# Spreading an expert's rows over the slots of its half in a top-2 mixture-of-experts block on one core

## The reference

```python
def hierarchical_moe(v, grp_w, grp_b, exp_w, exp_b, w_gate, w_up, w_down):
    ...
    grp_p, grp_idx = lax.top_k(grp_prob, 1)                  # 1 of 4 groups
    ...
    top_w, top_idx = lax.top_k(exp_prob, TOP_K_IN_GROUP)     # 2 of its 8 experts
    ...
        hg = jax.nn.silu(jnp.einsum('td,edf->tef', t, w_gate[g])) * jnp.einsum('td,edf->tef', t, w_up[g])
        hg = hg * combine[:, g, :, None].astype(hg.dtype)
        out = out + jnp.einsum('tef,efd->td', hg, w_down[g]).astype(F32)
```

## Time and profile before

| | us |
|---|---|
| median of 3 runs | 512.49 (511.51 to 515.82) |
| the profiled execution, its span | 512.3 |
| PE busy | 477.8 |
| DVE busy | 232.3 |
| ACT busy | 169.8 |
| POOL busy | 149.9 |

### The profile page before, as it was taken

The page is one execution under the profiler, slowest core; times in us unless marked ns, Lnnn a source line. Parts: engine busy times, 40 slices in busy tenths (PEclk is TensorE's granted clock), DMA queues, the critical chain, the costliest instruction groups (busy, mean ns, idle before and its releaser), DMA issues.

```text
span 512.3 us, 7264 instructions
## 1 busy us (share of the span) xinstructions
PE 477.8 (93%) x2718; PEld 264.5 (52%) x2718; DVE 232.3 (45%) x683; ACT 169.8 (33%) x283; POOL 149.9 (29%) x136
## 2 busy tenths in 40 slices
PE   3799999999999999989999999987999997999993
PEld 3355555744854457655555555543454553444441
DVE  2899948999233258642222222220211211565525
ACT  6633576547442333111111111120122111214454
POOL 1079999614100001222222222220121210003250
PEclk9999999999999999999999999997999998999998
DMA  8874300399499986899999999999999996990022
GB/s 299 145 202 93 70 0 2 125 155 168 156 357 412 421 339 221 316 391 421 419 418 419 418 414 417 419 418 420 420 421 419 416 406 228 399 371 2 0 82 82
DMA packets 60140, 144.73 MB, mean 283 GB/s; under 512 B 27587, under 2 KB 36839, under 8 KB 47817
## 3 DMA queue, kind: packets, MB, share of 16 engines
q1 hardware_dynamic: 54504, 133.92, 71.0%
q0 software_dynamic: 5328, 10.31, 5.3%
q10 hardware_dynamic: 272, 0.04, 0.0%
HBM read 138.17 MB, written 14.19 MB: 297 GB/s over the span
## 4 chain that ended last, share of the span: by engine, by line
PE 69%; DMA 18%; SPq 5%; DVE 3%; issue 2%; ACT 2%; POOL 0%; DVEq 0%; POOLq 0%
PE bank L1653 63%; DMA ring<-in_exp_w_up_dram 6%; DMA big<-in_exp_w_up_dram 6%; DMA moe<-v_d,gidx_all 4%; SPq L388 3%; DMA pairs_d<-moe,sidx_all 2%; PE bank L2059 1%; PE bank L1753 1%; SPq L364 1%; PE bank L1743 1%; PE bank L2078 1%; PE bank L1916 1%; PE bank L2176 1%; DVE moe L922 1%; SPq L393 1%
## 5 line engine op out<-in xcount | busy, mean ns | idle before, releaser
L1653 PE MATMUL bank<-ring,moe 128*64 128x256 f32 (+2 forms) x848 | 112.0, 410 | 3.7 <-DMA ring<-in_exp_w_up_dram 3.2
L1653 PEld LDWEIGHTS bank<-ring,moe 128*64 128x64 f32 x848 | 60.8, 140 | 40.7 <-issue 15.6
L1579 POOL DMA_INDIRECT pairs_d<-moe,sidx_all x32 | 31.8, 993 | 155.0 <-PE bank L2059 78.9
L922 DVE TENSOR_TENSOR vrow<-moe,bank 64x128 f32<-64x128 f32 x64 | 18.7, 291 | 118.3 <-ACT moe L821 117.3
L1653 PE MATMUL bank<-ut,big 128*128 128x512 f32 x128 | 57.7, 597 | 1.2 <-ACT ut L562 1.2
L821 ACT ACTIVATE moe<-bank 64x256 f32<-64x256 f32 x32 | 12.1, 377 | 138.2 <-PE bank L1653 138.2
L550 ACT ACTIVATE moe<-bank 128x512 f32<-128x512 f32 (+1 forms) x65 | 36.5, 582 | 60.6 <-PE bank L1653 50.5
L1653 PE MATMUL bank<-ring,ut 128*128 128x512 f32 x128 | 55.7, 593 | 0.4 <-DVE ut L922 0.4
L1653 PE MATMUL bank<-big,moe 128*64 128x256 f32 (+1 forms) x264 | 43.2, 440 | 3.0 <-DMA big<-in_exp_w_up_dram 2.6
L922 DVE TENSOR_TENSOR ring<-ring,bank 128x64 f32<-128x64 f32 (+1 forms) x142 | 39.5, 278 | 2.8
L1653 PEld LDWEIGHTS bank<-ring,ut 128*128 128x128 f32 x128 | 24.0, 190 | 29.3 <-issue 29.3
(11 more groups left out here) (198 smaller groups left out, 616.8 us busy)
## 6 DMA issues: line engine op xcount, KB each, us to landing
ring<-in_exp_w_gate_dram SPq DMA_DIRECT2D x19, 1024.0 KB, 23.8
ring<-in_exp_w_down_dram SPq DMA_DIRECT2D x18, 1024.0 KB, 26.9
ring<-in_exp_w_up_dram SPq DMA_DIRECT2D x17, 1024.0 KB, 20.2
big<-in_exp_w_up_dram SPq DMA_DIRECT2D x7, 1024.0 KB, 20.1
big<-in_exp_w_down_dram SPq DMA_DIRECT2D x7, 1024.0 KB, 18.2
big<-in_exp_w_gate_dram SPq DMA_DIRECT2D x6, 1024.0 KB, 20.6
ut<-in_exp_w_up_dram SPq DMA_DIRECT2D x4, 1024.0 KB, 24.0
h<-in_exp_w_down_dram SPq DMA_DIRECT2D x4, 1024.0 KB, 23.0
```

Source lines behind the costliest of these rows:

```text
L922: return dve.tensor_tensor(o, a, b, op)
L1579: pool.indirect_dma_start(pairs, bass.IndirectOffsetOnAxis(ap=index, axis=0), at(moe, ALL, M_Y + k * 512, [[1, 512]]), None, bounds_check= ...
L1653: return pe.matmul(o, a, b, start=start, stop=stop, skip_group_check=loose)
```

## The change

Another rank stands in each slot. Slot s = 8b + a (a and b from 0 to 7) held rank 8b + a and now holds rank 8a + b; so rank r stands in slot 8 (r mod 8) + r div 8. It is the same for both halves of the partitions. An expert with 32 rows filled slots 0 to 31; now it fills the first four slots of each run of eight: 0 to 3, 8 to 11, and so on to 56 to 59. Shapes, instructions, their order, the number of rows moved and every wait are the same. The index tables, X1, X30 and X31 come out of the same instructions with other contents.

```diff
     half = (np.arange(P) // CAP).astype(np.float32)[:, None]
-    place = np.broadcast_to((np.arange(P) % CAP).astype(np.float32), (P, P))
+    at_rank = np.arange(CAP).reshape(8, CAP // 8).T.reshape(-1)
+    place = np.broadcast_to(np.tile(at_rank, 2).astype(np.float32), (P, P))
```

## The result

| | before | changed |
|---|---|---|
| median of 4 runs, us | 514.14 (511.51 to 515.82) | 523.28 (522.25 to 524.08) |
| span of the profiled execution, us | 512.3 | 522.2 |
| ratio to before, 95% interval | | 1.0176 [1.0142, 1.021] |

The changed kernel is 9.1 us slower: slower by over 1%, inside the range of 515 to 525 us, 3.5 us above the forecast of 519.8. Of these 3.5 us some 1.6 come from the starting point (the forecast built on 512.5 us, the four runs of before have 514.14) and 1.8 from the change itself (+9.1 where +7.3 was forecast).

A forecast was written before the change was run, and what follows sets the result against it. The slowest DMA engine was taken to bound the stretch from 217 to 427 us. More rows on it, +7.6 us, and fewer empty packets, -0.3, gave +7.3 on 512.5: 519.8 us, range 515 to 525.

The forecast's parts named there:

- The bound: From 217 to 427 us all 16 DMA engines work without a gap; the slowest engine's sum is the length.
- -0.3 us for empty packets: On the slowest engine, rows replace some 35 empty packets at 0.01 us each: -0.3 us.
- No cover, no slack behind: Neither PE's work nor anything behind the last up piece's landing takes up its delay of 7.3 us.
- The last piece at 433 to 436 us: The chain's last DMA piece, expert 31's up piece, lands at 433 to 436 us instead of 427.4.
- The share well under 1 in the stretch: From 217 to 427 us the DMA share falls well under 1, from 1.02, as odd engines stand idle.
- Fewer engines in the first 0.3 us of a scatter: A scatter's first 0.3 us has full q0 packets from only 8 engines, where 12 were read before.
- Gathers a little longer than 9.2 us: Single gathers take a little longer than 9.2 us to land, at most 0.6 us, hidden early in the stretch.
- Rival 1: PE's clock stays at 1.2 GHz for its last experts, making the kernel slower still: 523 to 525 us, chance 0.06.
- the forecast's own 517.5 to 523: Range of the main forecast alone, 519.8 us, held to cover 0.7, before widening to 515 and 525.
- Rivals 2 and 3: Eight adjacent slots per engine, 495 us, chance 0.04; runs of four, second round backwards, 511 us, chance 0.07.
- the dealing: Runs of four slots dealt round: engine k has slots 4k to 4k+3 and 32+4k to 35+4k.
- Rival 4: Another limit than the slowest engine holds the landings, so its lag is made up: no change, 512.5 us, chance 0.11.

The follow-up runs named there:

- second trace: The changed kernel measured once more, nothing altered, against the kernel before: 523.43 us against 513.74, ratio 1.0198.
- the kernel with engine 0 heavy: Kernel before, with ranks 0 to 7 in engine 0's slots of either half, the rest dealt over the other seven: 523.55 us, 1.0194.
- engine 1, 2, 4 or 6 heavy: Kernel before, with ranks 0 to 7 in that one engine's slots of either half: 526.25, 526.24, 526.57 and 526.55 us against 514.26.

## Why the prediction was nearly right

**The bound.** All 16 engines without a gap from 217 to 427 us, and the slowest engine's sum as the length: right. With 2 of 16 engines heavy the kernel loses as much as with eight.

**-0.3 us for empty packets.** Too small to be tested.

**No cover, no slack behind.** Right: the tail from the landing is 85.1 us against 84.9. POOL, DVE, ACT and the table of constants cost nothing: their busy times are within 0.5 us.

**What the profile was to show.** The last piece at 433 to 436 us: it came at 437.1 (436.4 in the second trace). The share well under 1 in the stretch: yes, but only 0.91 and 0.96, since the light engines, which I had over 30 us ahead, can be ahead by no more than the queue holds: 22.5 us from the first engine's end to the last's. Idle at the end, 8 engines: yes. Fewer engines in the first 0.3 us of a scatter: the one of expert 6 has 0.02 MB of q0 there, where the earlier trace rows has 0.05 for another expert; 8 engines with a full packet each would be 0.03, so it fits but does not prove. Gathers a little longer than 9.2 us: no, 9.2 again; only the longest went from 9.9 to 10.9.

**The rivals.** Rival 1 (PE's clock): the landing is followed by 3.4 us at a granted clock of 0.50, the lower level, as before, and the 6.86 us became 7.08; 0.2 us, not 3.5. The time that it named, 523 to 525 us, was right for another reason. And that is where luck comes in: the 523.28 us lie just outside the forecast's own 517.5 to 523, and inside the whole range only because room was left for this rival, whose mechanism did not act. Rivals 2 and 3 fell with the dealing. Rival 4 (the lag is made up) fell with the kernel with engine 0 heavy: 14 engines stood still for some microseconds and the two others went on at 25 GB/s each.

## What to carry to other kernels

Where DMA engines are full, a transfer's cost is that of its slowest engine: count the filled rows per engine over the whole stretch under the dealing in runs of four, 4k to 4k + 3 and 32 + 4k to 35 + 4k for engine k, and let consecutive ranks go to different engines (`4 * (r % 8) + r // 8 % 4 + 32 * (r // 32)`; 508.2 us instead of 513.7 here). "Spread the rows out" is no goal in itself: with a stride of eight and half-filled slots it put all rows on half of the engines. Leave the balance once another chain sets the end; here the last scatter and the load behind it took over at about 1%. And leave room for what no table of rows shows: which engine was the heavy one made another 2.3 us at the same KB.

## What the runs showed of the hardware

- One DMA engine of a half with 944 KB of rows beside the even weights holds up a kernel with 14 others idle: a DMA share of 0.15, 61 GB/s, 25 GB/s for each engine at work (the kernel with engine 0 heavy). Others' idle time does not help it.
- The lead that light engines can have is bounded: 20 to 23 us at the last down piece in the kernels with heavy engines and all gathers, with some 31 us from a load's issue to its landing. Once the queue is full, SP's issues of 1 MB take mostly 2.1 us, and up to 10.7 in the changed kernel, instead of 0.33.
- Fetching instructions (16 KB, about 1.1 us of one engine) costs nothing on an engine with slack. Steps of some 2 us, of which 1.0 to 1.8 last, stand behind the fetches that fall, by their order, on a heavy one: by this reading engine 0 heavy is +9.8 us and engine 1, 2, 4 or 6 heavy is +12.0 to +12.3 at the same KB. The Trainium skill, page DMA: Bandwidth & Descriptors, section "Queues, rings and completion order", has each engine take its queues in turn, a packet at a time; by that a fetch would cost its own packet, 1.1 us. The traces agree with the order of size and have mostly somewhat more, for a reason that is not shown.
